# Decoder trunk on one core: the slots of the rounded weights in five layouts, and one slot's tokens streamed backwards

## The chip, the cores and the metric

The kernel runs on one core of a Trainium2 chip. The time is the device time of one execution in microseconds; the times shown below are medians over executions, and the trace comes from one profiled execution. Engines are named as the profile names them: PE is TensorE's matrix multiply and PEld its loading of weights (the stationary operand), DVE is VectorE, ACT is ScalarE, POOL is GpSimd, SP is the engine that issues the loads from DRAM.

## What is computed

Two decoder layers over 272 tokens (16 learned ones and 256 of the input), model width 1024, in float32:

```python
def swiglu_ffn(h, w_in, w_out):
    gate, up = jnp.split(h @ w_in, 2, axis=-1)
    return (jax.nn.silu(gate) * up) @ w_out

for i in range(DEPTH):                                  # DEPTH = 2
    h = layer_norm(DEEPNORM_ALPHA * h + 0.5 * swiglu_ffn(h, ffn_w_in[i, 0], ffn_w_out[i, 0]), ...)
    mix = short_conv_mixer(h, ...) if i % 2 == 0 else gla_mixer(h, ...)
    h = layer_norm(DEEPNORM_ALPHA * h + mix, ...)
    h = layer_norm(DEEPNORM_ALPHA * h + 0.5 * swiglu_ffn(h, ffn_w_in[i, 1], ffn_w_out[i, 1]), ...)
return h[:, N_META:]
```

The four FFNs (1024 to 2 x 2816 and back) hold most of the work; layer 0 has a short gated convolution between them and layer 1 a chunked gated linear attention (GLA).

## The kernel before

**Units.** All large weights are cut into 335 units of 128 partitions x 8 blocks x 128 columns, float32 (512 KB). A unit is one 128-wide strip of output features with up to 8 blocks of the contraction dimension; of the projection back from an FFN every third unit has 6 blocks, and the last FFN's 22 units of that projection (from `OUT_UNIT` = 313 on) are one contraction block with all 1024 output features.

**Three products for one.** Each float32 factor is kept as a rounded part ("hi", type float32r) and a remainder ("lo"), and a product is made as hi·hi + lo·hi + hi·lo. A unit goes through four steps:

- SP loads it into `raw`, a ring of `RAW` = 4 slots (L275); it waits until the remainder of the unit four before is made.
- ACT rounds it into `w_hi` (`split_hi`, L462). The ring of `w_hi` and `w_lo` has `RING` = 8 slots, unit n in slot n % 8; ACT waits until PE has used unit n - 8.
- DVE subtracts it from the raw weights into `w_lo` (`split_lo`, L821); POOL does this for unit 0 (L341).
- PE multiplies. In `multiply` (L1298) a unit takes 24 matmuls: 8 with `w_hi` and the hi activations (L1306), 8 with `w_lo` (L1309), 8 with `w_hi` and the lo activations (L1311). Each matmul loads a block of 128 x 128 weights as its stationary operand and streams 272 tokens past it (256 from the middle of the GLA stage on) into a PSUM bank. Where operands come late, a second form in `multiply` takes hi, lo and w_lo block by block (L1325 to L1327), as `multiply_raw` does for the first four units behind a norm (L1350 to L1352).

**The last projection** turns the roles round (`accumulate`, L1466): the stationary operand is a block of activations (128 tokens), and 512 columns of the unit's weights stream past it, 12 matmuls to a unit (L1469 to L1471).

**Order.** Every engine's order is written out by hand. DVE and ACT have the splits of later units between the work on the activations: per pair of units of an FFN, SiLU on ACT, product, rounding and remainder on DVE; at the norms and in GLA a good deal more. The token areas `x_hi` and `x_lo` are padded so that their rows start at certain distances.

**Layout.** In each slot of `w_hi` and `w_lo` the 1024 words of a partition lie side by side in the order (block, column), so ACT and DVE write, and PE reads, neighbouring words everywhere.

Of the kernel before, what the change touches and what calls it, by code (L numbers as in the profile page):

```python
# [19 lines left out]
F32 = mybir.dt.float32  # L20
F32R = mybir.dt.float32r
ALU = mybir.AluOpType
ACT = mybir.ActivationFunctionType

P = 128
LN_EPS = 1e-5
RMS_EPS = 1e-6
RAW = 4
RING = 8
KU = 8  # L30
# [3 lines left out]
def hybrid_trunk(nc, x, meta_tokens, ln_gain, ln_bias, ffn_w_in, ffn_w_out, conv_w_in, conv_w,  # L34
                 conv_w_out, gla_w_in, gla_w_gate_up, gla_b_gate, gla_norm_w, gla_w_out, out):
    _, SEQ, D = x.shape
    META = meta_tokens.shape[0]
    DEPTH = ln_gain.shape[0]
# [4 lines left out]
    KD = D // P  # L43
# [36 lines left out]
    with ctx:  # L80
        def sb(name, shape, dt=F32):
            return ctx.enter_context(nc.sbuf_tensor(name, shape, dt))

        def sem(name):
            return ctx.enter_context(nc.semaphore(name))

        raw = sb("raw_weights", [P, RAW, KU * P])
        w_hi = sb("weights_hi", [P, RING, KU * P], F32R)
        w_lo = sb("weights_lo", [P, RING, KU * P], F32R)
        x_hi_area = sb("x_hi", [P, KD, T + 16], F32R)  # L90
        x_lo_area = sb("x_lo", [P, KD, T + 48], F32R)
        x_hi, x_lo = x_hi_area[:, :, 0:T], x_lo_area[:, :, 0:T]

        def close_packed(area):
            words = area[:].rearrange("p k t -> p (k t)")
            return words[:, CLOSE_AT:CLOSE_AT + KD * SEQ].rearrange("p (k t) -> p k t", k=KD)
# [30 lines left out]
        with ExitStack() as inner:  # L127
            mid_hi = inner.enter_context(nc.sbuf_tensor("mid_hi", [P, KF, T], F32R))
            mid_lo = inner.enter_context(nc.sbuf_tensor("mid_lo", [P, KF, T], F32R))
        with ExitStack() as first:  # L130
# [3 lines left out]
            count = first.enter_context(nc.sbuf_tensor("count", [P, 512], mybir.dt.int32))  # L134
# [57 lines left out]
        hi_split, lo_split, unit_used = sem("hi_split"), sem("lo_split"), sem("unit_used")  # L192
# [134 lines left out]
        def _(pool):  # L327
# [6 lines left out]
            for source in (ln_gain.rearrange("l s (k p) -> (l s k) p", p=P),  # L334
# [3 lines left out]
                pool.dma_start(const_rows[row:row + source.shape[0], :], source).then_inc(rows_landed, 16)  # L338
                row += source.shape[0]
            pool.wait_ge(hi_split, 1)  # L340
            nc.gpsimd.tensor_tensor(w_lo[:, 0, :], raw[:, 0, :], w_hi[:, 0, :].bitcast(F32),  # L341
                                    ALU.subtract).then_inc(lo_split, 1)
            pool.wait_ge(gate_zeroed, 1)
            pool.dma_start(gate_up[0:RANK, :], gla_w_gate_up[0]).then_inc(gate_landed, 16)
# [111 lines left out]
        def _(act):  # L456
            def split_hi(n):

                if n >= RING:
                    act.wait_ge(unit_used, n + 1 - RING)  # L460
                act.wait_ge(raw_landed[n % RAW], (n // RAW + 1) * 16)
                nc.scalar.activation(w_hi[:, n % RING, :], raw[:, n % RAW, :], ACT.Copy).then_inc(hi_split, 1)  # L462

            def square_chunk(q, mo, n_tok):

# [350 lines left out]
        def _(dve):  # L816
            def split_lo(n):

                dve.wait_ge(hi_split, n + 1)
                s = n % RING  # L820
                nc.vector.tensor_tensor(w_lo[:, s, :], raw[:, n % RAW, :], w_hi[:, s, :].bitcast(F32),  # L821
                                        ALU.subtract).then_inc(lo_split, 1)

            def take_shift(q, mo, n_tok):
# [81 lines left out]
            def normalise(q, n_tok, late=None, early=None):  # L906
# [39 lines left out]
                if early is None:  # L946
                    split_lo(late + RING)
# [347 lines left out]
        @block.tensor  # L1295
        def _(pe):
            def block_of(w, n, k):
                return w[:, n % RING, k * P:(k + 1) * P]  # L1298

            def multiply(ps, n, source, cols, k0=0, k1=KU, first=True, last=True, ready=None, before_last=None, middles=()):  # L1300

                hi, lo = source
                if ready is None and before_last is None and not middles:
                    pe.wait_ge(hi_split, n + 1)
                    for k in range(k0, k1):
                        nc.tensor.matmul(ps, block_of(w_hi, n, k - k0), hi[:, k, cols], start=first and k == k0, stop=False)  # L1306
                    pe.wait_ge(lo_split, n + 1)
                    for k in range(k0, k1):
                        nc.tensor.matmul(ps, block_of(w_lo, n, k - k0), hi[:, k, cols], start=False, stop=False)  # L1309
                    for k in range(k0, k1):  # L1310
                        mm = nc.tensor.matmul(ps, block_of(w_hi, n, k - k0), lo[:, k, cols], start=False,  # L1311
                                              stop=last and k == k1 - 1)
                    mm.then_inc(unit_used, 1)
                    return
                pe.wait_ge(lo_split, n + 1)
                for k in range(k0, k1):
                    if ready is not None:
                        pe.wait_ge(ready[0], ready[1] + k + 1)
                    if before_last is not None and k == k1 - 1:
                        before_last()  # L1320
                    for at, extra in middles:
                        if k == at:
                            extra()
                    w_h, w_l = block_of(w_hi, n, k - k0), block_of(w_lo, n, k - k0)
                    nc.tensor.matmul(ps, w_h, hi[:, k, cols], start=first and k == k0, stop=False)  # L1325
                    nc.tensor.matmul(ps, w_h, lo[:, k, cols], start=False, stop=False)  # L1326
                    mm = nc.tensor.matmul(ps, w_l, hi[:, k, cols], start=False, stop=last and k == k1 - 1)  # L1327
                mm.then_inc(unit_used, 1)
# [73 lines left out]
            def ffn(f, n0, n_tok, q):  # L1402
# [3 lines left out]
                def tile(t, ready=None):  # L1406
                    g = KF * f + t
                    if t >= PAIRS:
                        pe.wait_ge(mid_ready, g - PAIRS + 1)
                    for half in range(2):  # L1410
                        multiply(bank[2 * (t % PAIRS) + half][:, 0:n_tok], n0 + 2 * t + half, (in_hi, in_lo), cols,
                                 ready=ready if half == 0 else None)
# [41 lines left out]
            def last_projection():  # L1454

                def turn_residual():
                    pe.wait_ge(mid_ready, 4 * KF)
                    pe.wait_ge(resid_ready, KD * LAST_NORM)
                    for part in range(2 * TB):
                        b, half = part // 2, part % 2  # L1460
                        for k in range(KD // 2):
                            mm = nc.tensor.transpose(bank[part][:, k * P:(k + 1) * P],
                                                     resid[:, half * KD // 2 + k, META + b * P:META + (b + 1) * P], ident[:])
                        mm.then_inc(resid_turned, 1)

                def accumulate(k, b, half, first, last):  # L1466
                    toks, cols = slice(META + b * P, META + (b + 1) * P), slice(half * D // 2, (half + 1) * D // 2)
                    ps, slot = bank[4 + 2 * b + half][:], (OUT_UNIT + k) % RING
                    nc.tensor.matmul(ps, mid_hi[:, k, toks], w_hi[:, slot, cols], start=first, stop=False)  # L1469
                    nc.tensor.matmul(ps, mid_hi[:, k, toks], w_lo[:, slot, cols], start=False, stop=False)  # L1470
                    return nc.tensor.matmul(ps, mid_lo[:, k, toks], w_hi[:, slot, cols], start=False, stop=last)  # L1471

                for k in range(KF - RING):
                    pe.wait_ge(lo_split, OUT_UNIT + k + 1)
                    pe.wait_ge(mid_ready, 3 * KF + k + 1)
                    for b in range(TB):
                        for half in range(2):
                            mm = accumulate(k, b, half, k == 0, False)
                    mm.then_inc(unit_used, 1)
                    if k == 2:  # L1480
                        turn_residual()
                for k in range(KF - RING, KF):
                    pe.wait_ge(lo_split, OUT_UNIT + k + 1)
                    for half in range(2):
                        mm = accumulate(k, 0, half, False, k == KF - 1)
                mm.then_inc(last_made, 2)
                for half in range(2):
                    for k in range(KF - RING, KF):
                        mm = accumulate(k, 1, half, False, k == KF - 1)
                    mm.then_inc(last_made, 1)  # L1490
# [111 lines left out]
            for j in range(4, GLA_TILES):  # L1602
# [3 lines left out]
                cols = main if short else every  # L1606
# [47 lines left out]
```

## Time and profile before

| | us |
|---|---|
| median of the runs | 1020.44 (1019.41 to 1021.48) |
| the profiled execution's time | 1018.82 |
| its span in the trace | 1017.1 |

| engine | busy us | share of the span |
|---|---|---|
| PE | 1004.7 | 99% |
| PEld | 983.9 | 97% |
| DVE | 723.6 | 71% |
| ACT | 512.4 | 50% |
| POOL | 122.2 | 12% |

The busy time of PE and PEld counts each instruction from its start to its modelled end, and these overlap, so the two shares do not say how far PE is from its peak. What one matmul costs is read from the distance between the starts of successive ones, that is from a stretch's length and the number of matmuls in it.

### The profile page before, as it was taken

Reading aid. Unit: us, or ns where it says so; the run is one execution under the profiler, and the core shown is the slowest. Engines: PE = TensorE matmul, PEld = TensorE weight load, DVE = VectorE, ACT = ScalarE, POOL = GpSimd, SP = SyncE. Lnnn points to the kernel's source line nnn. Section 1 sums busy time; section 2 is a strip of 40 time slices with the busy share of each in tenths; the row PEclk is TensorE's granted clock in tenths of the full one; section 3 lists DMA queues with packets and bytes.
Section 4 is the critical chain, followed back from the end, with each engine's and each line's share of the span. In section 5 each row is a group of like instructions: output and inputs, shape, how many; then the busy total and the mean of one; then the engine's idle time right before and its main releaser. Section 6 shows DMA issues by size and latency. Waiting matters only on the chain.

```text
span 1017.1 us, 18997 instructions
## 1 busy us (share of the span) xinstructions
PE 1004.7 (99%) x7866; PEld 983.9 (97%) x7866; DVE 723.6 (71%) x1078; ACT 512.4 (50%) x746; POOL 122.2 (12%) x136
## 2 busy tenths in 40 slices
PE   9999999999999999999999999999999999999997
PEld 7999999999999999999999999999989999999885
DVE  5865656689889865557697565667897999766444
ACT  5634344465456543444565434445867766444430
POOL 2000002320002000003220000133152420000000
PEclk9999999999999999999999999999999999999999
DMA  9965656637762966556639665555355738866531
GB/s 255 261 191 171 179 154 179 191 91 211 224 174 82 253 183 175 170 163 179 193 91 256 175 183 155 168 165 160 84 146 145 206 106 247 249 193 201 171 121 41
DMA packets 324263, 176.58 MB, mean 174 GB/s; under 512 B 6658, under 2 KB 320048, under 8 KB 324176
## 3 DMA queue, kind: packets, MB, share of 16 engines
q1 hardware_dynamic: 323664, 174.15, 59.3%
q8 instruction: 62, 1.02, 0.4%
q0 software_dynamic: 480, 1.15, 0.4%
q14 instruction: 25, 0.20, 0.1%
q10 hardware_dynamic: 32, 0.07, 0.0%
HBM read 174.29 MB, written 1.05 MB: 172 GB/s over the span
## 4 chain that ended last, share of the span: by engine, by line
PE 91%; DVE 4%; ACT 1%; issue 1%; POOL 1%; DMA 1%; SPq 0%; POOLq 0%; DVEq 0%; ACTq 0%
PE bank L1311 23%; PE bank L1306 23%; PE bank L1309 23%; PE bank L1325 3%; PE bank L1327 3%; PE bank L1326 3%; PE bank L1469 2%; PE bank L1471 2%; PE bank L1470 2%; PE bank L1350 2%; PE bank L1351 2%; PE bank L1352 2%; DVE weights_lo L821 1%; DMA raw_weights<-in_ffn_w_in_dram 1%; DVE rms L1219 1%
## 5 line engine op out<-in xcount | busy, mean ns | idle before, releaser
L462 ACT ACTIVATE weights_hi<-raw_weights 128x1024 fp32r<-128x1024 f32 x335 | 353.9, 1059 | 410.7 <-PE bank L1311 299.6
L821 DVE TENSOR_TENSOR weights_lo<-raw_weights,weights_hi 128x1024 fp32r<-128x1024 f32 x334 | 415.4, 1250 | 202.9 <-ACT weights_hi L462 201.7
L1306 PE MATMUL bank<-x_hi,weights_hi 128*128 128x272 f32 (+1 forms) x1584 | 226.5, 285 | 0.0
L1311 PE MATMUL bank<-x_lo,weights_hi 128*128 128x272 f32 (+1 forms) x1584 | 225.9, 285 | 0.0
L1309 PE MATMUL bank<-x_hi,weights_lo 128*128 128x272 f32 (+1 forms) x1584 | 223.9, 284 | 0.0
L1306 PEld LDWEIGHTS bank<-x_hi,weights_hi 128*128 128x128 f32 x1584 | 206.3, 188 | 0.6 <-ACT consts L628 0.2
L1311 PEld LDWEIGHTS bank<-x_lo,weights_hi 128*128 128x128 f32 x1584 | 206.9, 188 | 0.0
L1309 PEld LDWEIGHTS bank<-x_hi,weights_lo 128*128 128x128 f32 x1584 | 205.2, 188 | 0.0
L1306 PE MATMUL bank<-mid_hi,weights_hi 128*128 128x272 f32 x462 | 68.2, 288 | 0.0
L1309 PE MATMUL bank<-mid_hi,weights_lo 128*128 128x272 f32 x462 | 68.1, 288 | 0.0
L1311 PE MATMUL bank<-mid_lo,weights_hi 128*128 128x272 f32 x462 | 68.0, 288 | 0.0
L993 DVE TENSOR_TENSOR prod<-bank,silu_g 128x272 f32<-128x272 f32 (+1 forms) x82 | 35.7, 436 | 40.5 <-PE bank L1311 39.8
L1306 PEld LDWEIGHTS bank<-mid_hi,weights_hi 128*128 128x128 f32 x462 | 61.9, 188 | 0.0
L1309 PEld LDWEIGHTS bank<-mid_hi,weights_lo 128*128 128x128 f32 x462 | 61.8, 188 | 0.0
L1311 PEld LDWEIGHTS bank<-mid_lo,weights_hi 128*128 128x128 f32 x462 | 61.7, 188 | 0.0
L355 POOL TENSOR_TENSOR total<-resid 128x272 f32<-128x272 f32 x3 | 2.7, 907 | 429.8 <-DVE resid L850 429.8
L372 POOL TENSOR_TENSOR resid<-resid,mean 128x272 f32<-128x272 f32 (+1 forms) x40 | 32.7, 855 | 142.8 <-ACT mean L500 142.8
L1350 PE MATMUL bank<-zg_hi,weights_hi 128*128 128x274 f32 (+1 forms) x160 | 47.1, 295 | 0.0
L1352 PE MATMUL bank<-zg_hi,weights_lo 128*128 128x274 f32 (+1 forms) x160 | 46.0, 288 | 0.0
L1351 PE MATMUL bank<-zg_lo,weights_hi 128*128 128x274 f32 (+1 forms) x160 | 46.0, 288 | 0.0
L999 DVE TENSOR_TENSOR mid_lo<-prod,mid_hi 128x272 fp32r<-128x272 f32 (+1 forms) x88 | 38.6, 439 | 3.0
L1469 PE MATMUL bank<-weights_hi,mid_hi 128*128 128x512 f32 x88 | 35.0, 397 | 0.0
(231 smaller groups left out, 1197.8 us busy)
## 6 DMA issues: line engine op xcount, KB each, us to landing
raw_weights<-in_ffn_w_in_dram SPq DMA_DIRECT2D x176, 512.0 KB, 4.7
raw_weights<-in_ffn_w_out_dram SPq DMA_DIRECT2D x70, 512.0 KB, 4.2
raw_weights<-in_conv_w_in_dram SPq DMA_DIRECT2D x24, 512.0 KB, 4.0
raw_weights<-in_gla_w_in_dram SPq DMA_DIRECT2D x24, 512.0 KB, 3.9
raw_weights<-in_ffn_w_out_dram SPq DMA_DIRECT2D x24, 384.0 KB, 3.5
raw_weights<-in_conv_w_out_dram SPq DMA_DIRECT2D x8, 512.0 KB, 4.9
raw_weights<-in_gla_w_out_dram SPq DMA_DIRECT2D x8, 512.0 KB, 5.0
x_tok<-in_x_dram SPq DMA_DIRECT2D x2, 512.0 KB, 5.3
```

The costliest lines, as they stand in the source:

```text
L372: nc.gpsimd.tensor_tensor(resid[:, k, cols], resid[:, k, cols], mean[:, cols], ALU.subtract).then_inc(centred, 1)
L462: nc.scalar.activation(w_hi[:, n % RING, :], raw[:, n % RAW, :], ACT.Copy).then_inc(hi_split, 1)
L821: nc.vector.tensor_tensor(w_lo[:, s, :], raw[:, n % RAW, :], w_hi[:, s, :].bitcast(F32), ALU.subtract).then_inc(lo_split, 1)
L993: nc.vector.tensor_tensor(prod[:, s, cols], bank[2 * (t % PAIRS) + 1][:, 0:n_tok], silu_g[:, s, cols], ALU.mult).then_inc(prod_ready, 1)
L999: nc.vector.tensor_tensor(mid_lo[:, at_t, cols], prod[:, s:s + 1, cols], mid_hi[:, at_t, cols].bitcast(F32), ALU.subtract).then_inc(mid_re ...
L1306: nc.tensor.matmul(ps, block_of(w_hi, n, k - k0), hi[:, k, cols], start=first and k == k0, stop=False)
L1309: nc.tensor.matmul(ps, block_of(w_lo, n, k - k0), hi[:, k, cols], start=False, stop=False)
L1311: mm = nc.tensor.matmul(ps, block_of(w_hi, n, k - k0), lo[:, k, cols], start=False, stop=last and k == k1 - 1)
L1350: nc.tensor.matmul(ps, w_h, zg_hi[:, k, cols], start=k == 0, stop=False)
L1351: nc.tensor.matmul(ps, w_h, zg_lo[:, k, cols], start=False, stop=False)
L1352: mm = nc.tensor.matmul(ps, w_l, zg_hi[:, k, cols], start=False, stop=k == KD - 1)
L1469: nc.tensor.matmul(ps, mid_hi[:, k, toks], w_hi[:, slot, cols], start=first, stop=False)
```

## The change

One area `rounded` takes the place of `w_hi` and `w_lo`, of the same total size. It is cut into six pieces, each for one or two slots of the ring, and in a piece the hi and lo parts of its slots ("u", 2 or 4 of them) are laid out in an order of its own:

| slots | order | from one weight column to the next |
|---|---|---|
| 0, 1 | u, block, column | 1 word (4 bytes), as before |
| 2 | block, column, u (2) | 2 words (8 bytes) |
| 3, 4 | block, column, u (4) | 4 words (16 bytes) |
| 5 | column, u (2), block | 16 words (64 bytes) |
| 6, 7 | column, u (4), block | 32 words (128 bytes) |

All three engines go on taking the words in the order (block, column). So for slots 2 to 7 ACT writes its 1024 words one step apart, DVE reads the hi part and writes the lo part so, PE loads its 128 x 128 blocks so, and in the last projection streams 512 columns so. The raw weights stay side by side.

Besides, in the plain form of `multiply`, the units of slot 1 stream their tokens from the last to the first: both the activations read and the PSUM columns written have a step of -1 word.

No instruction is added, removed or moved on any engine and no wait is changed. There are as many matmuls, loads, roundings and subtractions as before, of as many elements, in the same order.

```diff
-        w_hi = sb("weights_hi", [P, RING, KU * P], F32R)
-        w_lo = sb("weights_lo", [P, RING, KU * P], F32R)
+        rounded = sb("rounded_weights", [P, 2 * RING * KU * P], F32R)
+        in_order = "p (u k m) -> p u k m"
+        LAYOUTS = [(0, 1, in_order), (1, 1, in_order), (2, 1, "p (k m u) -> p u k m"), (3, 2, "p (k m u) -> p u k m"),
+                   (5, 1, "p (m u k) -> p u k m"), (6, 2, "p (m u k) -> p u k m")]
+        w_hi, w_lo = [], []
+        for slot, count, order in LAYOUTS:
+            area = rounded[:, 2 * slot * KU * P:2 * (slot + count) * KU * P].rearrange(order, u=2 * count, k=KU, m=P)
+            for i in range(count):
+                w_hi.append(area[:, 2 * i, :, :])
+                w_lo.append(area[:, 2 * i + 1, :, :])
...
-                nc.scalar.activation(w_hi[:, n % RING, :], raw[:, n % RAW, :], ACT.Copy).then_inc(hi_split, 1)
+                nc.scalar.activation(w_hi[n % RING], in_blocks(raw[:, n % RAW, :]), ACT.Copy).then_inc(hi_split, 1)
...
-                nc.vector.tensor_tensor(w_lo[:, s, :], raw[:, n % RAW, :], w_hi[:, s, :].bitcast(F32),
+                nc.vector.tensor_tensor(w_lo[s], in_blocks(raw[:, n % RAW, :]), w_hi[s].bitcast(F32),
...
-                return w[:, n % RING, k * P:(k + 1) * P]
+                return w[n % RING][:, k, :]
...
                 if ready is None and before_last is None and not middles:
+                    if n % RING == 1:
+                        ps, cols = ps[:, ::-1], slice(cols.stop - 1, cols.start - 1 if cols.start else None, -1)
                     pe.wait_ge(hi_split, n + 1)
...
-                    nc.tensor.matmul(ps, mid_hi[:, k, toks], w_hi[:, slot, cols], start=first, stop=False)
-                    nc.tensor.matmul(ps, mid_hi[:, k, toks], w_lo[:, slot, cols], start=False, stop=False)
-                    return nc.tensor.matmul(ps, mid_lo[:, k, toks], w_hi[:, slot, cols], start=False, stop=last)
+                    nc.tensor.matmul(ps, mid_hi[:, k, toks], w_hi[slot][:, blocks, :], start=first, stop=False)
+                    nc.tensor.matmul(ps, mid_hi[:, k, toks], w_lo[slot][:, blocks, :], start=False, stop=False)
+                    return nc.tensor.matmul(ps, mid_lo[:, k, toks], w_hi[slot][:, blocks, :], start=False, stop=last)
```

## Rows read from the trace of the kernel before

**Rows 1.** The page: span, busy time by engine, busy tenths in 40 slices
```profile
span 1017.1 us, 18997 instructions
PE 1004.7 (99%) x7866; PEld 983.9 (97%) x7866; DVE 723.6 (71%) x1078; ACT 512.4 (50%) x746; POOL 122.2 (12%) x136
...
DVE  5865656689889865557697565667897999766444
ACT  5634344465456543444565434445867766444430
PEclk9999999999999999999999999999999999999999
```

**Rows 2.** The page: the chain that ended last, by engine
```profile
PE 91%; DVE 4%; ACT 1%; issue 1%; POOL 1%; DMA 1%; SPq 0%; POOLq 0%; DVEq 0%; ACTq 0%
```

**Rows 3.** Busy time by stretch, with counts; then granted clock and DMA
```profile
core 0: us, PE busy (x) PEld busy (x) DVE busy (x) ACT busy (x) POOL busy (x), PEclk, DMA share, GB/s
20.00:120.00 100.00, 100.00 (x806) 99.84 (x805) 66.03 (x93) 46.99 (x60) 0.00 (x0) 1.00 0.73 207
200.00:300.00 100.00, 100.00 (x798) 99.84 (x798) 87.87 (x151) 52.17 (x77) 9.28 (x10) 1.00 0.61 176
300.00:400.00 100.00, 100.00 (x799) 99.52 (x798) 76.93 (x123) 50.92 (x75) 6.50 (x8) 1.00 0.61 174
500.00:600.00 100.00, 100.00 (x802) 99.84 (x801) 73.39 (x114) 51.89 (x73) 7.03 (x9) 1.00 0.62 176
700.00:800.00 100.00, 97.76 (x778) 95.60 (x777) 84.99 (x126) 74.70 (x143) 40.07 (x52) 1.00 0.46 130
800.00:900.00 100.00, 99.40 (x856) 98.39 (x855) 85.62 (x146) 58.55 (x90) 8.66 (x11) 1.00 0.72 206
900.00:946.00 46.00, 46.00 (x408) 46.00 (x408) 29.12 (x42) 20.48 (x26) 0.00 (x0) 1.00 0.64 195
```

**Rows 4.** Timeline of PE, last projection: start, us, engine, line, operation, count
```profile
953.61 0.39 PE L1470 MATMUL bank<-weights_lo,mid_hi 128*128 128x512 f32 x1
953.84 0.40 PE L1471 MATMUL bank<-weights_hi,mid_lo 128*128 128x512 f32 x1
954.08 0.40 PE L1469 MATMUL bank<-weights_hi,mid_hi 128*128 128x512 f32 x1
954.31 0.39 PE L1470 MATMUL bank<-weights_lo,mid_hi 128*128 128x512 f32 x1
954.54 0.39 PE L1471 MATMUL bank<-weights_hi,mid_lo 128*128 128x512 f32 x1
954.78 1.91 PE L1462 MATMUL bank<-ident,resid 128*128 128x128 f32 x16
956.44 0.48 PE L1469 MATMUL bank<-weights_hi,mid_hi 128*128 128x512 f32 x1
```

**Rows 5.** The chain that ended last, a GLA score stage: start, us, what
```profile
755.78 1.41 PE bank L1569 x14
757.19 1.20 PE bank L1306 x8
```

**Rows 6.** Groups by line and form: busy, mean ns | idle before, releasers
```profile
L821 DVE TENSOR_TENSOR weights_lo<-raw_weights,weights_hi 128x1024 fp32r<-128x1024 f32 x334 | 415.4, 1250 | 202.9 <-ACT weights_hi L462 201.7 <-POOL weights_lo L341 0.7
L462 ACT ACTIVATE weights_hi<-raw_weights 128x1024 fp32r<-128x1024 f32 x335 | 353.9, 1059 | 410.7 <-PE bank L1311 299.6 <-DMA raw_weights<-in_ffn_w_in_dram 40.5 <-PE bank L1327 31.6
...
L889 DVE SCALAR_TENSOR_TENSOR zg_lo<-resid,consts,zg_hi 128x272 fp32r<-128x272 f32 x32 | 25.1, 783 | 0.0
```

**Rows 7.** The chain that ended last, end of GLA: start, us, what
```profile
783.82 6.17 DVE weights_lo L821 x4
...
795.73 4.15 DVE weights_lo L821 x3
...
800.69 1.76 DVE weights_lo L821
```

More of the change, by code:

```diff
@@ L92, in hybrid_trunk, with in_blocks @@
         x_hi, x_lo = x_hi_area[:, :, 0:T], x_lo_area[:, :, 0:T]
+        def in_blocks(unit):
+            return unit.rearrange("p (k m) -> p k m", m=P)
         def close_packed(area):
@@ L340, in _ @@
             pool.wait_ge(hi_split, 1)
-            nc.gpsimd.tensor_tensor(w_lo[:, 0, :], raw[:, 0, :], w_hi[:, 0, :].bitcast(F32),
+            nc.gpsimd.tensor_tensor(w_lo[0], in_blocks(raw[:, 0, :]), w_hi[0].bitcast(F32),
                                     ALU.subtract).then_inc(lo_split, 1)
@@ L1466, in accumulate @@
                 def accumulate(k, b, half, first, last):
-                    toks, cols = slice(META + b * P, META + (b + 1) * P), slice(half * D // 2, (half + 1) * D // 2)
+                    toks, blocks = slice(META + b * P, META + (b + 1) * P), slice(half * KD // 2, (half + 1) * KD // 2)
                     ps, slot = bank[4 + 2 * b + half][:], (OUT_UNIT + k) % RING
-                    nc.tensor.matmul(ps, mid_hi[:, k, toks], w_hi[:, slot, cols], start=first, stop=False)
-                    nc.tensor.matmul(ps, mid_hi[:, k, toks], w_lo[:, slot, cols], start=False, stop=False)
-                    return nc.tensor.matmul(ps, mid_lo[:, k, toks], w_hi[:, slot, cols], start=False, stop=last)
+                    nc.tensor.matmul(ps, mid_hi[:, k, toks], w_hi[slot][:, blocks, :], start=first, stop=False)
+                    nc.tensor.matmul(ps, mid_hi[:, k, toks], w_lo[slot][:, blocks, :], start=False, stop=False)
+                    return nc.tensor.matmul(ps, mid_lo[:, k, toks], w_hi[slot][:, blocks, :], start=False, stop=last)
                 for k in range(KF - RING):
```

## Prediction

> **What bounds the kernel now.** The profile's page comes first: PE is busy in every slice at full granted clock, DVE 71%, ACT 50% [rows 1], and PE carries 91% of the chain that ended last [rows 2]. So the time is the number of matmuls times the distance between their starts, and the question is what sets that distance: the stream of tokens or the weight load ahead of it.
>
> The stretches give it [rows 3]. From 20 to 120 us all matmuls stream 272 tokens, and 806 start in 100 us: one each 124.1 ns. From 900 to 946 us they stream 256, and 408 start in 46 us: 112.7 ns. In the last projection four starts of 512 columns take 953.61 to 954.54 us, 232.5 ns each [rows 4]. The distance follows the streamed columns, at about 0.45 ns each, so the stream is the bound and the load is hidden.
>
> How well it is hidden is the number that matters. Where little is streamed, the load shows. The 16 transposes stream 128 columns, which at 0.45 ns would take 58 ns, yet from 954.78 to 956.44 us one starts each 104 ns [rows 4]; the 14 score matmuls of 16 to 144 columns take 1.41 us, 101 ns each [rows 5]. Each loads a block of float32 of mostly 128 columns. I read from this that a load of 128 neighbouring words takes about 104 ns, 0.81 ns a word. Against 124.1 it has 20 ns of cover, a fifth of itself; against 112.7 only 9.
>
> **The change part by part.** Nothing is moved and no wait is new; only the price of a word can change, for four kinds of access.
>
> *1. Weight loads, slots 3 to 7 (16, 64 and 128 bytes from word to word).* Counting the units by n % 8 and kind, these slots have 4590 loads outside the last projection: 3630 with 272 tokens and 960 with 256. The trace of before has no load with a step, so the price has to be bounded (nor has it a split with one). From below: the load stays at 104 ns, or grows by less than the cover of 20 ns, and costs nothing. From above: it triples, 312 ns. The nearest measured ratio is inside the rows. The streamed operand gets a word each 0.45 ns, the load one each 0.81 ns, so the memory hands PE neighbouring words at nearly twice the pace at which a load takes them. If a fetch brings a pair of neighbours or more, a lone word wastes the rest of its fetch; a halved pace would make a load anywhere from 128 x 0.9 = 115 ns (only the spare pace is lost) to 208 ns (the load's own pace is halved). I take 208, because I know no reason why a load that takes one word at a time would have been built with a spare fetch, and the first would show as nothing. With 208 ns a load the load becomes the bound: 3630 x (208 - 124.1) = 305 us and 960 x (208 - 112.7) = 91 us, **+396 us**.
>
> The Trainium skill (Advanced Engine Details and Errata, SBUF Cachelines) says that the memory has lines of 16 bytes and that two accesses must fall into one line to hide its latency. By that rule slots 3 to 7, one word to a line, pay, and slot 2, two words to a line, does not; the trace of before can't show it, and this page of the Trainium skill has no price, so the sum by it is the one above.
>
> *2. Weight loads of slot 2 (8 bytes).* 726 loads with 272 tokens and 192 with 256. I take no loss: one neighbour is skipped, and what a fetch brings may still hold two wanted words. If it costs as much as the others, 726 x 83.9 + 192 x 95.3 ns = 79 us, and 8 us more in the last projection.
>
> *3. Streaming in the last projection.* Slots 3 to 7 have 14 of its 22 units, 168 matmuls of 512 columns at 232.5 ns. A stream already takes the memory's pace, so a lone word costs it at least double: +168 x 0.2325 = **+39 us**. If a word needs the 1.63 ns of a 208 ns load, 832 ns a matmul, it is +101 us. Nothing is the lower end. I take 39.
>
> *4. Tokens backwards, slot 1.* 774 matmuls in the plain form, 654 of 272 tokens and 120 of 256. Neighbours stay neighbours, the same pairs in the same fetches, only turned round; I take no loss. If pairing works upwards alone, on the reading or on PSUM's side, each doubles: 654 x 0.1241 + 120 x 0.1127 = 95 us.
>
> *5. Rounding on ACT and the remainder on DVE.* Now 1059 and 1250 ns for 1024 words, 1.03 and 1.22 ns a word [rows 6]. The slowest elementwise row of DVE nearby is the 272-word one of L889 with 783 ns, 2.88 ns a word [rows 6], which would make a split 2.95 us: that is the upper end, 1.25 the lower, and I take double, 2.5 us. In eight units that is 5 x 1.25 = 6.3 us more on DVE. Its cover is PE: with part 1 eight units take 3 x 24 x 0.1241 + 5 x 24 x 0.208 = 33.9 us of PE. In its busiest stretch, 200 to 300 us, DVE has 87.9 us for 798/24 = 33.3 units, 21.1 for eight [rows 3], so 27.4 with the new price, 29.6 at the upper end: hidden. ACT has 12.5 for eight there and gets 5.3 more: hidden too. At the end of GLA eight splits stand on the chain, 6.17 + 4.15 + 1.76 = 12.1 us [rows 7]; they would add 7.5, but PE's own work beside them is stretched by more. So nothing for this part, as long as part 1 holds; without that cover it decides (below).
>
> The Trainium skill (Vector Engine (DVE) Microarchitecture Reference, 5.2 Measured stream behaviour on trn2) gives DVE 2.50 ns a column instead of 1.05 where sources or output step by 24 words, and full pace only for pairs of adjacent words. By this rule a split would take about 2.6 us (an estimate from this page of the Trainium skill), near the doubled one, and slot 2, without adjacent pairs, would be slow as well; the sum changes by slot 2 alone, as rival 3 has it.
>
> **Sum.** 396 + 39 = 435 us on the profiled execution's span of 1017.1: 1452, and with the 1.7 us around it (1018.8 - 1017.1) **1454 us**. The profiled execution lies 1.6 us under the median of the runs, which is nothing here.
>
> **The rivals.**
>
> Rival 1: PE's reads cost nothing, and DVE becomes the bound in places. For it speaks the spare pace of part 1. Doubled splits in 5 of 8 slots add 33.3 x 5/8 x 1.25 = 26 us to 100 us of DVE: 114 instead of 88 from 200 us (14 over), 103 from 300 (3 over), 99 from 500, 110 from 700 (10 over), 113 from 800 (13 over), under 100 elsewhere [rows 3]. Together 41 us: 1060 us. With 2.95 us a split the excess is about 88 us, 1107; with 39 us for the last projection 1099 and 1146.
>
> Rival 2, on the other side: no change within 2%. The load must stay under 124 ns, the last projection's stream must keep its pace, and the splits must grow by under 0.6 us, so that only the stretch from 200 us is full. One mechanism does it: the memory hands out any word of a partition at one pace whatever its distance. Then all is as before, 1020 us. Against it: the kernel's streams already run at 0.45 and not at one pace with the load, so neighbours seem to be fetched together. Faster has no mechanism but noise.
>
> Rival 3: loads with 8 bytes cost as the others do, or backwards streams double, or both: 1454 + 88 = 1542, 1454 + 95 = 1549, 1637 with both.
>
> Rival 4: the distance counts beyond 16 bytes. If only slots 5 to 7 are slow (2178 and 576 loads, 96 streams), 183 + 55 + 22 = 260 us: 1279. If these take three times as long and slots 3 and 4 double, 2754 x 0.104 + 22 = 308 us more than the sum: 1762.
>
> Rival 5: the load slows by less than double. At 150 ns it is 3630 x 25.9 + 960 x 37.3 ns = 130 us, and 39 for the last projection: 1188.
>
> **How the numbers follow.** Doubled loads, with what of rivals 3 and 4 keeps it between 1270 and 1640 us: 0.52, the sum 1454 being its middle. Beyond that (threefold loads): 0.12. Rival 1: 0.20. Rival 5: 0.08. Rival 2: 0.08, of it 0.01 faster. The range of 1080 to 1700 leaves out rival 2 (0.08), about a third of rival 1 and under half of the threefold case, together 0.2. The likeliest case's own range is 1270 to 1640. A measurement of this kernel can tell about 2% from no change, and all cases but rival 2 lie above: slower 0.92, same 0.07, faster 0.01.
>
> **What would show it.** Units go round the slots, so the timeline after should show a pattern of period eight: three units of 2.98 us and five of about 5 us, the distance between loads 208 ns and the same for 272 and 256 tokens, with DVE and ACT waiting longer for PE than before. Splits should have two lengths, 1.25 and about 2.5 us. In the last projection 512-column matmuls should start 465 ns apart in slots 3 to 7. The units of slot 1 should look as those of slot 0. I am wrong if the distance in slots 3 to 7 stays at 124 ns; then the waits of PE for DVE say whether rival 1 holds. A slow slot 2 or slot 1 shows rival 3, differences among slots 3 to 7 rival 4.

## The result

The changed kernel takes 1545.36 us (median of 2 runs, 1545.35 to 1545.37) against 1020.44: 1.515 times, 95% interval 1.512 to 1.518. That is slower, inside the forecast range of 1080 to 1700 us, 91 us above the predicted 1454 and inside the likeliest case's own range. 434 us of loss were forecast and 525 were measured.

The page of the kernel after, beside [rows 1, 2] of the kernel before: parts 1 and 2 and the chain that ended last by engine.

```profile
span 1543.6 us, 18997 instructions
...
PE 1534.3 (99%) x7866; PEld 1476.1 (96%) x7866; DVE 892.8 (58%) x1078; ACT 720.3 (47%) x746; POOL 128.7 (8%) x136
...
PEclk9999999999999999999999999999999999999999
...
PE 99%; DVE 0%; POOL 0%; issue 0%; POOLq 0%
```

PE is busy in both, and its 7866 matmuls are the same ones, yet the chain is now PE's to 99% (91% before). DVE works 169 us more and matters less. The clock is full up to the last 7 us, as before, so no part of the loss is clock.

Busy time by stretch, in the columns of [rows 3] (its row from 20 us has 806 matmuls):

```profile
20.00:120.00 100.00, 100.00 (x504) 100.00 (x504) 58.44 (x60) 48.20 (x41) 0.00 (x0) 1.00 0.49 142
500.00:600.00 100.00, 100.00 (x538) 100.00 (x537) 51.67 (x56) 40.29 (x35) 0.00 (x0) 1.00 0.40 117
```

From 806 to 504 matmuls in 100 us: the mean distance went from 124 to 198 ns. The timeline of PE shows the forecast pattern (start, us, engine, line, operation, count). A unit is three rows of 8 matmuls (the third is left out here), and the units are 20 to 24, in slots 4, 5, 6, 7 and 0:

```profile
98.21 2.03 PE L1319 MATMUL bank<-x_hi,rounded_weights 128*128 128x272 f32 x8
100.07 2.03 PE L1322 MATMUL bank<-x_hi,rounded_weights 128*128 128x272 f32 x8
...
103.82 1.95 PE L1319 MATMUL bank<-x_hi,rounded_weights 128*128 128x272 f32 x8
105.60 1.95 PE L1322 MATMUL bank<-x_hi,rounded_weights 128*128 128x272 f32 x8
...
109.18 1.98 PE L1319 MATMUL bank<-x_hi,rounded_weights 128*128 128x272 f32 x8
110.99 1.99 PE L1322 MATMUL bank<-x_hi,rounded_weights 128*128 128x272 f32 x8
...
114.62 1.96 PE L1319 MATMUL bank<-x_hi,rounded_weights 128*128 128x272 f32 x8
116.42 1.96 PE L1322 MATMUL bank<-x_hi,rounded_weights 128*128 128x272 f32 x8
...
120.01 1.17 PE L1319 MATMUL bank<-x_hi,rounded_weights 128*128 128x272 f32 x8
121.01 1.16 PE L1322 MATMUL bank<-x_hi,rounded_weights 128*128 128x272 f32 x8
```

The starts of the rows are what to read, not their busy times. Eight matmuls take 1.86 us in slot 4 (16 bytes from word to word), 1.78 in slot 5 (64 bytes), 1.81 and 1.80 in slots 6 and 7 (128 bytes), and 1.00 in slot 0.

The 7632 matmuls with weights stand in the trace in the order of PE's program, which tells the unit of each, so each start can be given its slot. The medians of the distances, and the sums over all matmuls of a slot:

```
slot (step)     272 tokens, ns      256 tokens, ns     512 columns, ns     sum, us
                before   after      before   after     before   after      before   after
0 (4 B)          125      125        113      114       232      232       122.2    122.3
1 (4 B, back)    125      125        113      118       234      233       121.6    122.8
2 (8 B)          125      126        114      121       233      453       121.3    131.4
3 (16 B)         125      234        114      235       232      461       121.1    231.4
4 (16 B)         125      233        114      235       232      461       122.0    231.8
5 (64 B)         125      223        113      222       235      433       122.9    220.6
6 (128 B)        125      227        113      225       234      432       120.9    222.8
7 (128 B)        125      225        113      224       233      433       119.5    217.0
```

(The distance is that to the next start on PE. The 272 and 256 columns are of the plain form.) Slots 3 to 7 lose 517 us, slot 2 loses 10, slot 1 loses 1: together 528, and the span grew by 526.5. In slots 3 to 7 it no longer matters whether 272 or 256 tokens are streamed: the load sets the distance.

The timeline of PE in the last projection, at the border of unit 327 (slot 7) and unit 328 (slot 0), answers to [rows 4]:

```profile
1500.27 0.61 PE L1483 MATMUL bank<-rounded_weights,mid_hi 128*128 128x512 f32 x1
1500.71 0.61 PE L1484 MATMUL bank<-rounded_weights,mid_lo 128*128 128x512 f32 x1
1501.14 0.41 PE L1482 MATMUL bank<-rounded_weights,mid_hi 128*128 128x512 f32 x1
1501.38 0.39 PE L1483 MATMUL bank<-rounded_weights,mid_hi 128*128 128x512 f32 x1
```

From start to start a matmul of slot 7 takes 0.43 to 0.44 us, the first of slot 0 0.24 (medians 0.433 and 0.232).

### The profile page after: what moved, and what is told of

Read it like the earlier page. It is cut to its first block, busy times and chain, and to the rows that moved or that the text cites. A ratio compares the mean times of both kernels' runs of the same rounds, so it can differ in the third digit from the quotient of the medians.

```text
span 1543.6 us, 18997 instructions
## 1 busy us (share of the span) xinstructions
PE 1534.3 (99%) x7866; PEld 1476.1 (96%) x7866; DVE 892.8 (58%) x1078; ACT 720.3 (47%) x746; POOL 128.7 (8%) x136
## 3 DMA queue, kind: packets, MB, share of 16 engines
q0 software_dynamic: 480, 1.15, 0.3%
## 4 chain that ended last, share of the span: by engine, by line
PE 99%; DVE 0%; POOL 0%; issue 0%; POOLq 0%
PE bank L1319 25%; PE bank L1322 25%; PE bank L1324 25%; PE bank L1339 3%; PE bank L1338 3%; PE bank L1340 3%; PE bank L1483 2%; PE bank L1482 2%; PE bank L1484 2%; PE bank L1365 2%; PE bank L1364 2%; PE bank L1363 2%; PE bank L1582 0%; PE bank L1465 0%; PE bank L1600 0%; PE bank L1525 0%
## 5 line engine op out<-in xcount | busy, mean ns | idle before, releaser
L473 ACT ACTIVATE rounded_weights<-raw_weights 128x1024 fp32r<-128x1024 f32 x335 | 566.8, 1698 | 666.6 <-PE bank L1324 564.2
L832 DVE TENSOR_TENSOR rounded_weights<-raw_weights,rounded_weights 128x1024 fp32r<-128x1024 f32 x334 | 578.4, 1742 | 436.7 <-ACT rounded_weights L473 435.3
L1319 PE MATMUL bank<-x_hi,rounded_weights 128*128 128x272 f32 (+1 forms) x1584 | 332.6, 352 | 0.0
L1322 PE MATMUL bank<-x_hi,rounded_weights 128*128 128x272 f32 (+1 forms) x1584 | 331.5, 352 | 0.0
L1324 PE MATMUL bank<-x_lo,rounded_weights 128*128 128x272 f32 (+1 forms) x1584 | 330.8, 351 | 0.0
L1319 PEld LDWEIGHTS bank<-x_hi,rounded_weights 128*128 128x128 f32 x1584 | 315.5, 273 | 0.3
L1322 PEld LDWEIGHTS bank<-x_hi,rounded_weights 128*128 128x128 f32 x1584 | 315.7, 273 | 0.0
L1324 PEld LDWEIGHTS bank<-x_lo,rounded_weights 128*128 128x128 f32 x1584 | 315.3, 273 | 0.0
L1319 PE MATMUL bank<-mid_hi,rounded_weights 128*128 128x272 f32 x462 | 97.9, 353 | 0.0
L1322 PE MATMUL bank<-mid_hi,rounded_weights 128*128 128x272 f32 x462 | 97.7, 352 | 0.0
L1319 PEld LDWEIGHTS bank<-mid_hi,rounded_weights 128*128 128x128 f32 x462 | 92.7, 272 | 0.0
L1322 PEld LDWEIGHTS bank<-mid_hi,rounded_weights 128*128 128x128 f32 x462 | 92.7, 273 | 0.0
L1363 PE MATMUL bank<-zg_hi,rounded_weights 128*128 128x274 f32 (+1 forms) x160 | 59.9, 374 | 0.0
L1365 PE MATMUL bank<-zg_hi,rounded_weights 128*128 128x274 f32 (+1 forms) x160 | 59.2, 370 | 0.0
L1483 PE MATMUL bank<-rounded_weights,mid_hi 128*128 128x512 f32 x88 | 50.9, 578 | 0.0
L1482 PE MATMUL bank<-rounded_weights,mid_hi 128*128 128x512 f32 x88 | 50.9, 578 | 0.0
```

The source lines that it names most:

```text
L473: nc.scalar.activation(w_hi[n % RING], in_blocks(raw[:, n % RAW, :]), ACT.Copy).then_inc(hi_split, 1)
L832: nc.vector.tensor_tensor(w_lo[s], in_blocks(raw[:, n % RAW, :]), w_hi[s].bitcast(F32), ALU.subtract).then_inc(lo_split, 1)
L1363: nc.tensor.matmul(ps, w_h, zg_hi[:, k, cols], start=k == 0, stop=False)
L1365: mm = nc.tensor.matmul(ps, w_l, zg_hi[:, k, cols], start=False, stop=k == KD - 1)
L1482: nc.tensor.matmul(ps, mid_hi[:, k, toks], w_hi[slot][:, blocks, :], start=first, stop=False)
L1483: nc.tensor.matmul(ps, mid_hi[:, k, toks], w_lo[slot][:, blocks, :], start=False, stop=False)
```

## Experiments

Two questions were left by the result. Is the cause PE's reads alone, or do the slower writes of ACT and DVE take part? And why does a load take 223 to 235 ns and not 208: is it more by itself, or does the stream beside it add to it?

### Only the writes stepped

ACT and DVE write stepped in slots 3 to 7, PE reads neighbours (the weights PE reads stand in another order then).

```diff
+        STEP = (1, 1, 1, 4, 4, 8, 8, 8)
...
+        def stepped(w, s):
+            return w[:, s, :].rearrange("p (h m l) -> p h l m", l=STEP[s], m=P)
...
-                nc.scalar.activation(w_hi[:, n % RING, :], raw[:, n % RAW, :], ACT.Copy).then_inc(hi_split, 1)
+                nc.scalar.activation(stepped(w_hi, n % RING), blocks(raw[:, n % RAW, :], n % RING), ACT.Copy).then_inc(hi_split, 1)
```

(and the same on DVE; `blocks` is the matching view of the raw weights)

> The kernel before, but ACT and DVE write (and DVE reads the hi part) with a step in slots 3 to 7 (4 words in slots 3 and 4, 8 words in slots 5 to 7, each part within its own 4 KB), while PE goes on reading neighbouring words. The weights that PE reads stand in another order, so the output is not the reference's; the number and shape of all instructions is. Theory (PE's reads are the cause): splits of about 2.04 us on DVE and 2.05 us on ACT in slots 3 to 7, 1.22 and 1.06 us in the others; the distance between matmuls stays at 125 ns; the whole takes 1020 to 1040 us, because DVE gets 33.3 x 5/8 x 0.81 = 17 us more work per 100 us, which overfills only the stretches from 200 us (88 + 17) and 800 us (86 + 18). Rival (the slower writes hold the weights back, or disturb PE's reads): over 1100 us, PE waiting for DVE, or matmul distances over 130 ns.

Measured: 1056.9 us, 1.037 times the kernel before (1.034 to 1.039). PE's median distance stays at 125 ns. The theory holds on the cause, since 36 us are a fifteenth of the loss, but its 1020 to 1040 us were too few. The stretches, and one short one inside the first, show where the rest is (columns as [rows 3]):

```profile
200.00:300.00 100.00, 93.65 (x715) 92.95 (x714) 95.93 (x132) 64.27 (x65) 12.18 (x11) 0.95 0.57 163
285.00:292.00 7.00, 5.13 (x21) 4.81 (x21) 6.82 (x11) 3.36 (x4) 0.00 (x0) 0.52 0.63 186
...
400.00:500.00 100.00, 100.00 (x804) 100.00 (x804) 82.95 (x84) 68.76 (x55) 12.30 (x7) 1.00 0.60 173
...
800.00:900.00 100.00, 89.93 (x727) 87.70 (x727) 86.61 (x122) 75.60 (x101) 24.20 (x26) 0.97 0.49 143
```

Where DVE has few other tasks (400 us) nothing is lost. In the stretch from 200 us it is nearly full (96%) and PE does 715 matmuls instead of 798. From 800 us DVE is at 87% and not full, and the kernel still falls back (the 727 matmuls can't be set against the 856 of before, since this kernel is 23 us late by then and the stretch holds other work). There it is not DVE's total that counts but, as far as the waits show, that each split comes later in a hand-written order in which rounding, remainder and the work on the activations wait for each other: before one matmul in the GLA stage PE waits 6.1 us for POOL, before one at the end of the convolution 3.6 for ACT. And the clock takes a part. After such waits the granted clock falls to 1.2 GHz for some microseconds (0.52 from 285 to 292 us, 0.985 over the whole); the 92 matmuls with weights that start there take 21 us, 10 more than at full clock. The splits also cost more than the expectation took: 2.06 us on DVE at 16 bytes, but 2.29 to 2.32 at 32 bytes (medians by slot, counted as above). This kernel is rival 1 of the prediction, made real (with 32 bytes in slots 5 to 7).

### Only the loads stepped

```diff
             def block_of(w, n, k):
-                return w[:, n % RING, k * P:(k + 1) * P]
+                s = n % RING
+                return stepped(w, s)[:, k // STEP[s], k % STEP[s], :]
```

The same steps, for PE's loads alone; ACT and DVE write neighbours, the last projection streams neighbours.

> The kernel before, but the weight loads of the matmuls outside the last projection step through slots 3 to 7 (4 words in slots 3 and 4, 8 words in 5 to 7), while ACT and DVE write neighbouring words and the last projection streams neighbouring words. The blocks that PE reads hold the weights in another order, so the output is not the reference's. Theory (each load of lone words takes about 228 ns): distances of 225 to 235 ns in slots 3 to 7 for both 272 and 256 tokens, and 1020 + (1545 - 1020) less 46 us for the last projection = about 1495 us. Rival (part of the loss comes from the stepped writes of ACT and DVE running beside PE): distances nearer 208 ns, 1020 + 396 = 1416 us or less.

Measured: 1545.9 us (1.516 times, 1.512 to 1.520), with distances of 233 ns in slots 3 and 4 and 241 to 242 in slots 5 to 7. Without any stepped write, slots 3 and 4 load as slowly as in the changed kernel (233 to 234): the writes of ACT and DVE have no part in it. That the total equals the changed kernel's is chance: the last projection's loss is missing, and 32 bytes cost 17 ns a load more than 64 and 128 bytes did, which for 2754 loads is the 46 us that the expectation took off. The expectation of 1495 us had not separated the steps.

### Slots 3 and 4 undone

```diff
-        LAYOUTS = [(0, 1, in_order), (1, 1, in_order), (2, 1, "p (k m u) -> p u k m"), (3, 2, "p (k m u) -> p u k m"),
+        LAYOUTS = [(0, 1, in_order), (1, 1, in_order), (2, 1, "p (k m u) -> p u k m"), (3, 2, in_order),
```

> The changed kernel with slots 3 and 4 (16 bytes from word to word) laid out in neighbouring words again. Theory (the losses of the slots add up): these two slots took 231.4 + 231.8 us of PE's distances and 121.1 + 122.0 before, so 220 us come back: 1325 us. Rival (the bound moves to DVE, ACT or the loads of the other slots once these are fast): less comes back, over 1340 us.

Measured: 1329.4 us (1327.7 to 1331.1), 216 us less than the changed kernel, where 220 were expected. Slots 3 and 4 are back at 121.7 and 122.7 us, and the others keep their sums to within 2 us. The losses of the slots add up, and no other bound comes up behind them.

### All tokens backwards

```diff
                 if ready is None and before_last is None and not middles:
+                    ps, cols = ps[:, ::-1], slice(cols.stop - 1, cols.start - 1 if cols.start else None, -1)
```

> The kernel before, with the tokens streamed backwards in the units of all slots (plain form of multiply), not of one. Theory (backwards costs nothing): 1020 us, or up to 1026 if the 256-token units start 118 instead of 113 ns apart as those of slot 1 did (1200 x 4.5 ns = 5 us). Rival (a backwards stream is slow, but slot 1 hid it): over 1040 us.

Measured: 1.0033 times (1.0014 to 1.0051), 3 us. Streams of 272 tokens backwards start 124 ns apart; those of 256 start 118 apart instead of 113, and that covers the whole difference. Turning is not the only thing that brings these 118 ns: in the kernel with only the loads stepped, the 256-token streams of slots 0 to 2, forwards and on weights side by side, start 118 ns apart too. In the kernel before these streams stand on packed rows at chosen distances; what costs them 4 or 5 ns was not settled. Step 4 of the prediction holds.

### Steps from 1 to 8 words, and loads without cover

Each slot loads at a step of its own, and the second eight matmuls of each unit stream 64 tokens, so that the load is not hidden; the last projection streams in eight ways.

```diff
+SHORT = 64
...
+                row, s = w[:, n % RING, :], n % RING
+                step = (1, 2, 3, 4, 5, 6, 8, 7)[s]
+                return row[:, k:k + 127 * step + 1:step]
...
-                        nc.tensor.matmul(ps, block_of(w_lo, n, k - k0), hi[:, k, cols], start=False, stop=False)
+                        nc.tensor.matmul(ps[:, 0:SHORT], block_of(w_lo, n, k - k0),
+                                         hi[:, k, cols.start:cols.start + SHORT], start=False, stop=False)
```

> The kernel before, with the slots of the ring each loading weights at a step of its own: 1, 2, 3, 4, 5, 6, 8 and 7 words in slots 0 to 7 (writes stay side by side). The second eight matmuls of each plain unit (those with the lo weights) stream 64 tokens instead of all, so that their distance shows the load itself. In the last projection each slot streams its 512 columns in a way of its own: 0 straight, 1 read backwards alone, 2 step 2, 3 step 4, 4 step 8, 5 pairs of neighbours 4 words apart, 6 four neighbours 8 words apart, 7 written backwards alone. The output is not the reference's, since PE reads the weights in another order and leaves out tokens of the lo weights. Theory 1 (a load of lone words costs 1.78 ns a word of itself): beside 64 tokens the loads take 104 ns at step 1 and 2, and about 228 ns at 4 words and more, as beside 272; step 3 between, near 166, since two of its three 16-byte lines hold one word. Theory 2 (a lone word costs twice the load's pace, 208 ns, and the stream beside it adds 20): beside 64 tokens about 208 ns, beside 272 about 228. In the last projection: step 4 and 8 at 461 and 433 to 461 ns, step 2 at 453, pairs and fours at 232 if a fetch brings two neighbours, backwards at 232.

The second sweep has other first words, and 16 tokens in place of 64:

```diff
+SHORT = 16
...
+                row, s = w[:, n % RING, :], n % RING
+                step, first = ((1, 0), (1, 1), (2, 0), (2, 1), (4, 0), (4, 2), (8, 0), (3, 0))[s]
+                at = first + k // 4 * 4
+                return row[:, at:at + 127 * step + 1:step]
```

> As the sweep of steps, with loads (step, first word modulo 4) of (1,0), (1,1), (2,0), (2,1), (4,0), (4,2), (8,0), (3,0) in slots 0 to 7, and 16 tokens in the second eight matmuls. In the last projection: 0, 6 and 7 straight, straight, straight but slot 6 reads backwards at step 2; 1 both read and written backwards; 2 step 2 from an odd word; 3 pairs of neighbours from an odd word, 510 columns; 4 four neighbours from word 2 of a 16-byte line, 508 columns; 5 pairs 8 words apart. The output is not the reference's, for the same reasons. Theory 1: the second eight matmuls start 104 ns apart at steps 1 and 2 whatever the first word, about 228 ns at 4 and 8, beside 16 tokens as beside 64. Theory 2: 208 ns or less at 4 and 8. If a fetch is an aligned pair, streams in pairs from an odd word take up to double (465 ns) and pairs from an even word 232; if a fetch is a whole line of 16 bytes, step 2 would have been fast.

These two kernels did not keep the full clock, which the page of the first shows (the row of the granted clock, in tenths), and one of its stretches, in which PE is busy throughout:

```profile
PEclk9777788897899877787888777978879997777899
```
```profile
20.00:120.00 100.00, 100.00 (x485) 100.00 (x484) 42.41 (x58) 30.01 (x38) 0.00 (x0) 0.79 0.49 139
```

So their total times (1652 and 1454 us) say nothing, but the distances can be sorted by the granted level at the time. Medians in ns, of matmuls with the same level at both starts ("-": under 9 of them). The first word is its place in a line of 16 bytes in the second sweep; in the first, which the rows with (0) hold as well, it goes through all four places:

```
load, step (first word)   beside 16 or 64 tokens      beside 272 tokens
                          2.4 GHz     1.2 GHz         2.4 GHz     1.2 GHz
1 word (0)                112         213 to 214      126         227
1 word (1)                112         -               126         -
2 words (0)               118 to 119  213             126 to 127  227
2 words (1)               118         -               125         -
3 words                   173 to 175  213             175 to 176  227
4 words (0)               233         -               234         234 to 240
4 words (2)               233         233             235         239
5 words                   221         220             226         227
6 words                   224         223             228         227
7 words                   231         230             235         233
8 words                   238         238             242 to 243  241 to 242
```

Theory 1 holds in kind and theory 2 falls: a load at 4 words takes 233 ns beside 16 tokens, 233 beside 64 and 234 beside 272. The stream adds 1 ns there and 4 or 5 at 5 to 8 words, not 20.

What was wrong is the other end. A load of neighbouring words, uncovered, takes 112 ns here, and not the 104 and 101 that the transposes and score products showed [rows 4, 5]. Those are products of the plain float32 type and these of the rounded one; whether this is the difference was not tested. Twice 112 is 224, and the measured 221 to 238 ns lie around it.

The steps up to 4 words fit a price per line of 16 bytes, an estimate that takes 1.83 ns from the load at 4 words. At 1.83 ns a line, 128 words at step 4 touch 128 lines (234 ns, measured 233), at step 3 they touch 96 (176, measured 173 to 175), at step 2 they touch 64 (117, measured 118 to 119), and at step 1 only 32, which would be 59 ns: there something else, the words themselves perhaps, sets 112. The Trainium skill (Advanced Engine Details and Errata, SBUF Cachelines) asks for two accesses to a line of 16 bytes, and for loads the trace agrees but for a little: two to a line cost 7 ns, one to a line 121. Both clock levels say that the two prices are of different kinds: at 1.2 GHz the neighbours' load goes from 112 to 213 ns, the one at 4 words stays at 233. The price of a line doesn't follow TensorE's clock.

Beyond 16 bytes, with 128 lines each time, it is not the same for all steps: 221 at 20 bytes, 224 at 24, 238 at 32, and 223 to 227 at 64 and 128 in the changed kernel.

The streams of 512 columns in the last projection, medians:

```
straight, or read backwards, or written backwards, or both   232 to 233 ns
four neighbours 8 words apart, on a line of 16 bytes         234
four neighbours (508 columns) from the middle of a line      449
pairs 4 words apart                                          453
pairs from an odd word (510 columns)                         450
pairs 8 words apart                                          461
step 2; step 2 from an odd word; step 2 backwards            453; 453; 466
step 4; step 8                                               461; 431
```

The expectation that pairs would be enough fell. Of the patterns tried, a stream keeps its pace straight, in either direction, and in whole, aligned groups of four neighbours, and everything else goes at about half, pairs hardly better or worse than lone words. The stream's rule is thus not the load's: at step 2 a load loses 7 ns of 112, a stream half its pace. The page of the Trainium skill named above makes no such difference, and here the measurement decides.

### All slots at 8 bytes

```diff
-        LAYOUTS = [(0, 1, in_order), (1, 1, in_order), (2, 1, "p (k m u) -> p u k m"), (3, 2, "p (k m u) -> p u k m"),
-                   (5, 1, "p (m u k) -> p u k m"), (6, 2, "p (m u k) -> p u k m")]
+        LAYOUTS = [(s, 1, "p (k m u) -> p u k m") for s in range(RING)]
```

> The changed kernel (with slot 1 still streamed backwards) with all eight slots laid out as slot 2: 8 bytes from word to word, in the loads, in the stream of the last projection and for ACT and DVE. Theory (a load takes the longer of 0.875 ns a word and 1.83 ns a line of 16 bytes, so 112 ns at one word and 119 at two; a stream that is not of whole aligned fours of neighbours takes 0.88 ns a word): the loads stay hidden behind 272 tokens (126 ns) and reach 121 ns behind 256; the last projection takes 264 x 220 = 58 us more; with 1536 x 6 and 5800 x 1.2 ns for the rest, about 1020 + 58 + 9 + 7 = 1094 us. Rival (loads of 8-byte steps were hidden in slot 2 only because its neighbours in the ring were slow or fast ones): over 1150 us.

Measured: 1092.9 us, 1.073 times (1.070 to 1.075), where 1094 was expected. The loads stay hidden behind 272 tokens (124 to 126 ns), show a little behind 256 (121, in the backwards slot 118), and the last projection's matmuls start 453 ns apart in all slots. This is the price list of the sweeps put to a timed use.

### Short streams, no step

```diff
+SHORT = 64
...
-                        nc.tensor.matmul(ps, block_of(w_lo, n, k - k0), hi[:, k, cols], start=False, stop=False)
+                        nc.tensor.matmul(ps[:, 0:SHORT], block_of(w_lo, n, k - k0),
+                                         hi[:, k, cols.start:cols.start + SHORT], start=False, stop=False)
```

> The kernel before, all weights side by side, with the second eight matmuls of each plain unit on 64 tokens instead of all (tokens of the lo weights are left out, so the output is not the reference's). Theory (a load of neighbouring words takes 112 ns and is not hidden behind 64 tokens): 112 ns from start to start in these, 125 and 114 in the others; 2046 matmuls x 12 ns less than before, about 995 us, if the clock stays at full. Rival (the sweeps lost granted clock, 0.84 and 0.86, because of these short streams and not because of the stepped loads): granted clock well under 1.00, and so distances of 226 ns in the long streams and over 1100 us.

Measured: 999.5 us (0.981 times, 0.979 to 0.983) where about 995 was expected, with the expected 111 to 112 ns between the short matmuls, and this stretch of it at full clock:

```profile
20.00:120.00 100.00, 99.96 (x832) 99.74 (x831) 67.83 (x94) 49.03 (x62) 0.00 (x0) 1.00 0.74 211
```

A third of the matmuls on 64 tokens does not cost the clock, nor do loads at 4 and 8 words with full streams:

```profile
core 0: 1544.0 us, clock 0.998
```

That is the kernel with only the loads stepped. Both together, as in the sweeps, brought 0.84 (64 tokens) and 0.86 (16 tokens). Streams of 16 tokens without a step were not run, and why the two together lower the clock stays open.

## The prediction, step by step

**What bounds the kernel** held: the stream, with the load hidden behind it. The cover was smaller than thought, 12 ns and not 20 behind 272 tokens (124.1 - 112), and next to nothing behind 256 (112.7 - 112).

**1, loads of slots 3 to 7: right in kind, the term too small.** The step that failed is "I read from this that a load of 128 neighbouring words takes about 104 ns", from which 208 came. The load took 223 to 235 ns by slot. Of the 517 us that slots 3 to 7 lost, the last projection has 168 x 0.21 = 35, so the loads lost 482 where 396 were forecast. Those 86 us are nearly all of the missing 91. With the uncovered load of these very matmuls, 112 ns, the doubling would have given 224 and 3630 x 99.9 + 960 x 111.3 ns = 469 us.

The factor of two was the right choice for a reason that the prediction did not have, and its fit is in part luck. It was argued as a halved pace of the load. The sweeps show two prices of different kinds, 112 ns for neighbours, which follows TensorE's clock (213 at 1.2 GHz), and 233 at 4 words, which does not; that one is about twice the other holds at 2.4 GHz alone. Nor does a lone word halve the pace by missing its neighbour, since 8 bytes, which skip every neighbour, take 118 ns; by the fit above it counts how many of its words share 16 bytes.

**2, loads of slot 2: right.** 126 ns behind 272 tokens; what it lost beside its stream is 2 us.

**3, the stream of the last projection: right for slots 3 to 7**, 35 us measured and 39 forecast. It was missed that the same stream in slot 2, which was given no loss, doubles too: 36 x 0.22 = 8 us. The text had assigned these 8 us to rival 3, as if load and stream had one rule for 8 bytes. They have two.

**4, backwards: right**, 1 us in slot 1 and 3 us in all slots.

**5, ACT and DVE: right that it is hidden.** The groups of the splits, in the columns of [rows 6]:

```profile
L473 ACT ACTIVATE rounded_weights<-raw_weights 128x1024 fp32r<-128x1024 f32 x335 | 566.8, 1698 | 666.6 <-PE bank L1324 564.2 <-PE bank L1340 45.6 <-PE bank L1484 44.2
L832 DVE TENSOR_TENSOR rounded_weights<-raw_weights,rounded_weights 128x1024 fp32r<-128x1024 f32 x334 | 578.4, 1742 | 436.7 <-ACT rounded_weights L473 435.3
```

ACT's idle time before a rounding, most of which ends with PE, grew from 411 to 667 us, and DVE's before a split from 203 to 437: both have more room than before, not less. By slot a split takes 1.22 us in slots 0 to 2 and 1.94 to 2.06 in slots 3 to 7 (2.5 were taken), a rounding 1.06, 1.15 in slot 2, and 2.00 to 2.13 (double). The Trainium skill (Vector Engine (DVE) Microarchitecture Reference, 5.2 Measured stream behaviour on trn2) has 2.50 ns a column for steps of 24 words, and asks for adjacent pairs; here 64 bytes take 1.9 ns a word and 8 bytes nothing on DVE.

**The rivals.** That the total lies by the 1542 and 1549 us of rival 3 is chance: neither the loads at 8 bytes nor the backwards streams are slow. This could be told from the slots' rows alone, not from the total. Rival 1's price, 1060 us without the last projection, was near what its mechanism does when nothing covers it (1057), but by a balance of errors: splits taken longer than they are, and the waits inside the hand-written order and the lower clock after them not counted. Rival 2's mechanism, one pace for any word, is excluded, and so are rival 5's 150 ns and the order of sizes in rival 4: 16 bytes cost no less than 64 and 128.

## What to carry to other kernels

Where a matmul's stream hides its weight load, measure the cover on the same kind of matmul with a short stream before changing how weights lie: here the load had 12 ns of cover and grew by 111 to 123, which added half of the run time again. Weights that TensorE loads may lie 8 bytes apart in float32 for 7 ns a load, whereas what it streams should lie side by side, in either direction, or at least in whole aligned groups of four neighbours. And when a total meets a rival's number, look whether its mechanism is in the rows.

## What was not expected of the hardware

- Loads and streams follow different rules. A load up to 4 words' step fits a price by lines (1.83 ns each, once that exceeds 112 ns in all), a stream took either 0.45 or 0.84 to 0.91 ns a word, and of the groups tried aligned fours alone kept the first.
- The time of a load of lone words is the same at 2.4 and at 1.2 GHz (233 ns at 4 words), so at the lower clock, where a neighbours' load takes 213 ns, the step costs 20 ns and not 121.
- 32 bytes from word to word are the slowest step tried, for loads (238 to 242 ns, 64 and 128 bytes 223 to 227) and for ACT and DVE (2.3 us a unit, 16, 64 and 128 bytes 1.9 to 2.1). Why was not tried.
- With PE busy throughout, the granted clock fell only where stepped loads and short streams came together (0.84, 0.86), and not with stepped loads alone (0.998) or streams of 64 tokens alone (0.999). The changed kernel itself, with its matmuls 198 ns apart in place of 124, kept the full clock. With only the writes stepped it fell after PE had waited several microseconds (0.985 over the whole).
